# Hymba-style decoder layer on 8 cores: K, V and the forget logits of the first four chunks from an unnormalised x

## The reference, cut to what matters

```
h = rmsnorm(x) * g_mix_pre                     # norm over the 1024 channels
[a_val | a_gate | q | k | v | f_logit] = h @ w_in      # 512 | 512 | 512 | 512 | 512 | 8
A = silu(layernorm(depthwise_conv31(a_val * sigmoid(a_gate))))
B = softmax(q k^T / 8 + sum of log_sigmoid(f_logit + b_forget) over (s, t]) v     # causal, 8 heads x 64
x = x + rmsnorm([A, B] @ w_out)
x = x + rmsnorm((silu(h2 @ w_gate) * (h2 @ w_up)) @ w_down)      # h2 = rmsnorm(x), d_ff 2816
```

## Time and profile before

| | |
|---|---|
| median of 3 runs | 2460.57 us (2458.22 to 2514.89) |
| the profiled execution, its own time | 2455.3 us |
| its span, slowest core (core 7) | 2453.8 us |
| spans of the 8 cores | 2444.3 to 2453.8 us |
| granted TensorE clock, mean | 0.978 |
| busy share: TensorE / ScalarE / VectorE / GpSimd | 92% / 64% / 43% / 21% |

### The profile page before, as it was taken

The page is one execution under the profiler, slowest core; times in us unless marked ns, Lnnn a source line. Parts: engine busy times, 40 slices in busy tenths (PEclk is TensorE's granted clock), DMA queues, the critical chain, the costliest instruction groups (busy, mean ns, idle before and its releaser), DMA issues.

```text
span 2453.8 us, 53606 instructions; the slowest of 8 cores (2444.3 to 2453.8 us)
## 1 busy us (share of the span) xinstructions
PE 2264.7 (92%) x19730; PEld 1078.8 (44%) x19730; DVE 1044.1 (43%) x1638; ACT 1577.3 (64%) x1395; POOL 523.7 (21%) x887
## 2 busy tenths in 40 slices
PE   7988989999999798999999999999999999999895
PEld 3443444444444343444444444444444444444342
DVE  3545455555453533433344243324433432444633
ACT  2246676786776776776777777677777777762211
POOL 0222322322222201230131132023013101302301
PEclk9999999999999899999999999999999999999997
DMA  6766767758769667356445635635563664554542
GB/s 157 192 160 134 187 154 176 186 137 206 164 122 205 159 167 186 108 150 199 129 126 179 178 110 154 206 108 144 165 185 99 169 190 112 151 170 139 160 142 92
DMA packets 226220, 383.76 MB, mean 156 GB/s; under 512 B 34736, under 2 KB 153776, under 8 KB 223920
## 3 DMA queue, kind: packets, MB, share of 16 engines
q1 hardware_dynamic: 192736, 295.98, 42.2%
q0 software_dynamic: 33232, 84.34, 17.1%
HBM read 350.19 MB, written 72.02 MB: 172 GB/s over the span
## 4 chain that ended last, share of the span: by engine, by line
PE 66%; ACT 11%; issue 7%; DVE 7%; DMA 3%; POOL 3%; SPq 1%; DVEq 0%; ACTq 0%; POOLq 0%
PE pbig L470 66%; ACT s_pt L1243 5%; SPq L435 1%; DMA s_kr<-k_s 1%; DVE s_hT L570 1%; ACT s_sq L587 1%; ACT L486 1%; DMA s_xs<-xT 1%; DVE s_tmp L1008 1%; POOL s_pt L1252 1%; ACT s_pt L1248 1%; DVE s_vst L684 1%; ACT s_rstd L486 1%; DMA conv_s<-s_cvst 1%; POOL s_ssA L511 1%
## 5 line engine op out<-in xcount | busy, mean ns | idle before, releaser
L1243 ACT ACTIVATE s_pt<-pbig,s_bias 128x2048 bf16<-128x2048 f32 x512 | 1007.1, 1967 | 426.9 <-PE pbig L470 409.6
L470 PE MATMUL pbig<-s_h,s_wr 128*128 128x512 bf16 x2816 | 671.5, 382 | 15.1 <-DVE s_sa L1075 14.8
L470 PEld LDWEIGHTS pbig<-s_vr,s_pt 128*128 128x128 bf16 x8832 | 345.6, 98 | 167.9 <-issue 48.5
L470 PEld LDWEIGHTS pbig<-s_h,s_wr 128*128 128x128 bf16 x2816 | 253.7, 98 | 375.4 <-issue 119.9
L470 PE MATMUL pbig<-s_vr,s_pt 128*128 128x65 bf16 x8832 | 367.2, 194 | 22.6 <-DVE s_atok L1283 9.8
L470 PE MATMUL pbig<-s_qr,s_kr 64*128 64x512 bf16 x1024 | 308.4, 381 | 60.9 <-ACT s_pt L1243 46.0
L1075 DVE SCALAR_TENSOR_TENSOR s_sa<-s_th,pbig 128x512 f32<-128x512 f32 x176 | 120.9, 687 | 494.8 <-ACT s_th L1074 428.8
L470 PE MATMUL pbig<-s_qw,s_kr 64*128 64x512 bf16 x1024 | 309.9, 383 | 0.0
L1252 POOL TENSOR_SCALAR_AFFINE_SELECT s_pt<-s_pt 128x128 bf16<-128x128 bf16 x256 | 89.6, 350 | 826.5 <-ACT s_pt L1248 792.7
L470 PE MATMUL pbig<-s_actA,s_wr 128*128 128x512 bf16 x1024 | 257.8, 383 | 0.2 <-DVE s_sa L1075 0.2
L511 POOL TENSOR_TENSOR s_ssA<-s_ssA,s_sqr 128x512 f32<-128x512 f32 x98 | 131.6, 1342 | 463.0 <-ACT s_sqr L504 459.2
(11 more groups left out here) (153 smaller groups left out, 2291.3 us busy)
## 6 DMA issues: line engine op xcount, KB each, us to landing
s_wr<-wg_b SPq DMA_DIRECT2D x88, 512.0 KB, 4.0
s_wr<-wu_b SPq DMA_DIRECT2D x88, 512.0 KB, 4.6
s_wr<-wd_b SPq DMA_DIRECT2D x128, 352.0 KB, 3.2
s_vr<-v_s SPq DMA_DIRECT2D x288, 130.0 KB, 3.5
s_kr<-k_s SPq DMA_DIRECT2D x448, 64.0 KB, 3.7
s_xs<-xT POOLq DMA_DIRECT2D x48, 512.0 KB, 7.8
s_u<-u_s POOLq DMA_DIRECT2D x32, 540.0 KB, 12.1
s_x<-xT POOLq DMA_DIRECT2D x32, 512.0 KB, 5.6
```

The source lines that it names most:

```text
L470: P.op("pe", lambda e: e.matmul(out, lhsT=lhsT, rhs=rhs, start=start, stop=stop, **kw), reads=reads, writes=[wkey])
L1243: P.op("act", lambda e: e.activation(out=p[:], in_=pbig[:, 0:4, :], func=AF.Exp, bias=bias[:, c, h:h + 1], scale=1.0), reads=bk + bias.key ...
```

## The change

It does four things.

1. Chunks 0 to 3 get a path of their own, `p_raw`. hT is x * g without r, piece by piece as the pieces come. K is computed with the contraction outermost: for each piece k one matmul of squares and 4 of K, into 5 PSUM banks at once. r is applied when K, V, the logits (and Q and the gates of chunk 1, which reads the same hT) leave PSUM. V and logits have the tokens on partitions, so r is first turned into a column (`rows`: 4 small matmuls and a copy). For chunk 3 hT is made anew with r, for its Q and gates.
2. The K and V weights come in 8 pieces each, the gate weights in 4, and the host lays the gate columns out for that. x pieces of chunks 1 to 3 are loaded singly. vecs, tri and kmask go to ScalarE's queue.
3. The planner no longer counts a transfer that its engine has already waited for; `a_pump` fills one ring slot per step in the wait before a head group.
4. Matmuls that only pass the time: 29 instead of 38.

```diff
         for d in self._deps(eng, reads, writes):
             if d.is_dma:
-                t = max(t, self.landed[d.semkey])
+                if self.clock[eng].get(("dma", d.semkey), 0) < d.dma_n:
+                    t = max(t, self.landed[d.semkey])
...
+    def raw_in(i, k):
+        H = hT[i % 3]
+        P.op("act", lambda e: e.activation(out=sq[:, k, :], in_=xs[:, k, :], func=AF.Square), ...)
+        P.op("dve", lambda e: e.tensor_scalar(out=H[:, k, :], in0=xs[:, k, :], scalar1=V(V_GPRE + k), scalar2=None, op0=ALU.mult), ...)
+        if i + 1 < NRAW:
+            ld("sp", xs, xs[:, k:k + 1, :], xT_d[i + 1, :, k:k + 1, :], reads=winKV.keys[10 + k // 2:11 + k // 2] if i == 0 else (), ...)
+
+    def rows(r):
+        for tb in range(4):
+            mm(pb[0][:, tb:tb + 1], r[:, tb * 128:(tb + 1) * 128], tri[:, 0:1], True, True, r.keys + tri.keys, PB(0))
+        P.op("dve", lambda e: e.tensor_copy(out=rT[:], in_=pb[0][:, 0:4]), ...)
...
+    def p_raw(i, idle):
+        own, j, H, r = i % 2 == 1, i // 2, hT[i % 3], RAW[i]
+        for k in range(8):
+            if i == 0:
+                raw_in(0, k)
+            mm(pb[4][:], ones_bf[:], sq[:, k, :], k == 0, k == 7, ...)
+            for hp in range(4):
+                mm(pb[hp][:], winKV[:, k, hp * 128:hp * 128 + 128], H[:, k, :], k == 0, k == 7, ...)
+            if i == 0 and k < 7:
+                idle(3)
+            yield 5 * MM
+        norm_tail(4, r, 1.0 / D)
+        for hp in range(4):
+            P.op("dve", lambda e, hp=hp: e.tensor_tensor(out=kst[:, hp, :, i % 2, :], in0=pb[hp] ..., in1=r[:] ..., op=ALU.mult), ...)
...
+        else:
+            for tb in range(4):
+                b = bank()
+                yield from group(8, ...)              # V, as before
+                if tb == 1:
+                    rows(r)
+                    v_raw(W, V0, b0, 0)
+                    v_raw(W, V0, b, 1)
+                elif tb:
+                    v_raw(W, V0, b, tb)
+                b0 = b
+                if tb:
+                    for _ in range(2):
+                        if nxt:
+                            raw_in(*nxt.pop(0))
+        yield from logits(i, H, rT)
+        while nxt:
+            raw_in(*nxt.pop(0))
...
     def p_stream():
-        wl("k", winKV, 0, C_K, C_V)
-        for g in range(8):
-            ld("sp", xs, xs[:, g:g + 1, :], xT_d[0, :, g:g + 1, :], ...)
-        ld("sp", vecs, vecs[:], vecs_d)
+        ld("act", vecs, vecs[:], vecs_d)
+        for k in range(8):
+            ld("sp", xs, xs[:, k:k + 1, :], xT_d[0, :, k:k + 1, :], ...)
+        for k in range(8):
+            wk(k, 0, C_K, C_V, winKV.keys[k], ...)
+        for k in range(8):
+            wk(k, 512, C_V, DIN, winKV.keys[8 + k], ...)
...
-        yield from p_kv(0)
-        yield from p_kv(1)
-        flush_h(2)
-        wl("q", winQ, 0, C_Q, C_K, hT[2].keys[0:1])
-        wl("g", winG, 0, 0, C_Q, hT[2].keys[0:1])
+        for i in range(NRAW):
+            yield from p_raw(i, idle)
+            if i == 2:
+                wl("q", winQ, 0, C_Q, C_K, xs.keys[4:5])
+                for cb in range(4):
+                    P.dma("pool", ... winG[:, :, 256 * cb:256 * cb + 256] ..., reads=xs.keys[7:8], ...)
...
+        defer(("h", 3), [scale_by(xs, V_GPRE, rstd, hT[0], k) for k in range(8)], 2, 2)
...
     def gates(j, cb, H, r=None):
+        if r is not None:
+            P.op("dve", lambda e: e.tensor_tensor(out=T[:], in0=pb[bg][:], in1=r[:], op=ALU.mult), ...)
...
+        if r is not None:
+            P.op("dve", lambda e: e.tensor_tensor(out=U[:], in0=T[:], in1=r[:], op=ALU.mult), ...)
...
-            a_pump()
             t0 = fa[0]
             while fa[0] < min(t0 + 18.0, p_end[0]):
+                a_pump(1)
                 yield None
+            a_pump()
```

More of the change, by code:

```diff
@@ L274 @@
 MM = 512 / 2400.0
-EARLY = 1
+NRAW = 4
 NKV = 4
@@ L572, in scale_by @@
             reads=[src.keys[k]] + vecs.keys + r.keys, writes=[dst.keys[k]])
[L574 removed]
+    WK = {"k": lambda k: winKV.keys[k:k + 1], "v": lambda k: winKV.keys[8 + k:9 + k], "q": lambda k: winQ.keys}
+    GK = lambda cb: winG.keys[cb:cb + 1]
+    RAW = {0: rstd, 1: mean, 2: rstd, 3: rstd}
     def proj_T(H, W, c0, b, wk):
[L577 removed]
+        yield from group(8, lambda k: W[:, k, c0:c0 + 128], lambda k: H[:, k, :], pb[b][:], lambda k: (WK[wk](k) if type(wk) is str else wk) + [H.keys[k]], b)
     def flush_h(i):
@@ L588, in norm_sq @@
                                        reads=[xs.keys[k]], writes=[sq.keys[k]]), [xs.keys[k]], "act") for k in range(8)])
[L590 to L604, removed]
+    def raw_in(i, k):
+        H = hT[i % 3]
+        P.op("act", lambda e: e.activation(out=sq[:, k, :], in_=xs[:, k, :], func=AF.Square), reads=[xs.keys[k]], writes=[sq.keys[k]])
+        P.op("dve", lambda e: e.tensor_scalar(out=H[:, k, :], in0=xs[:, k, :], scalar1=V(V_GPRE + k), scalar2=None, op0=ALU.mult),
+             reads=[xs.keys[k]] + vecs.keys, writes=[H.keys[k]])
+        if i + 1 < NRAW:
+            ld("sp", xs, xs[:, k:k + 1, :], xT_d[i + 1, :, k:k + 1, :], reads=winKV.keys[10 + k // 2:11 + k // 2] if i == 0 else (),
+               keys=[xs.keys[k]], sem=("xs0", k))
@@ new lines, in v_fill, with logits @@
+    def v_fill(j, own):
+        W = vst_of(j)
+        if not own and j > 1:
+            P.op("dve", lambda e: e.memset(W[:, :, 4 if j < NOWN - 1 else 0:8, 64:65], 1.0), writes=W.keys)
+        return W, 0 if own else 4
+    def logits(i, H, r=None):
+        bf_ = bank()
+        o = 32 * (i % 2)
+        for tb in range(4):
+            yield from group(8, lambda k: H[:, k, tb * 128:(tb + 1) * 128], lambda k: winKV[:, k, 1024:1032],
+                             pb[bf_][:, tb * 8:tb * 8 + 8], lambda k: WK["v"](k) + [H.keys[k]], bf_, cost=0.033, step=8)
+        if r is None:
+            P.op("dve", lambda e: e.tensor_tensor(out=zt[:, o:o + 32], in0=pb[bf_][:, 0:32], in1=V(V_BF, 32), op=ALU.add),
+                 reads=[PB(bf_)] + vecs.keys, writes=zt.keys)
+            return
+        for tb in range(4):
+            a = o + 8 * tb
+            P.op("dve", lambda e, a=a, tb=tb: e.scalar_tensor_tensor(
+                out=zt[:, a:a + 8], in0=pb[bf_][:, 8 * tb:8 * tb + 8], scalar=r[:, tb:tb + 1], in1=V(V_BF + 8 * tb, 8), op0=ALU.mult, op1=ALU.add),
+                reads=[PB(bf_)] + vecs.keys + r.keys, writes=zt.keys)
@@ L966, in p_own @@
             for cb in range(4):
-                yield from gates(j, cb, H)
+                yield from gates(j, cb, H, r)
                 if cb == 0 and i == 5:
@@ L1188, in build_program, with a_pump @@
     un, uf, qn, qf = [0], [0], [0], [0]
-    def a_pump():
-        while True:
+    def a_pump(n=8):
+        for _ in range(n):
             did = False
```

134 lines of the change are left out of this document (79 added, 55 removed).

## The result

| | before | after |
|---|---|---|
| comparable runs | 2458 to 2461 us | 2431.31, 2435.04, 2437.91 us |
| ratio to before, 95% interval | 1 | 0.9898 [0.9879, 0.9918] |
| first K product of a chunk, mean | 23.8 us | 9.6 us |
| end of chunk 0's logits | 44.9 | 35.6 |
| first Q product | 108.2 | 90.9 |

The change gains 25 us, 1.0%; 2437 was forecast. In the profiled execution of the changed kernel one die's cores ran at a granted clock of 0.92 to 0.93, so it is read on the other die's cores, 4 to 7, and the means of after are over these; those of before and of the experiments are over all eight.

What follows compares the result with a forecast made beforehand. TensorE bounds the kernel (92% busy), with waits and half clock in the first chunks. First Q matmul 24.9 us earlier, less 1 for Q, gates and halo: 24 off 2455.3 gives 2431, plus 5.3 for the median: 2437 us; range 2423 to 2458.

Steps and rivals of the forecast that it cites:

- K of chunk 0: Start: K matmuls go along with the pieces; x and K weights there at about 20.1 us, K done at 22.0.
- B: Rival for the start: weights run ahead of x, x ends at 27.1 us; gain 16, 2444 us; chance 0.12.
- D: Rival: fast hT products on VectorE block GpSimd's descriptors, weights 5 to 6.6 us later; gain 18, 2443; chance 0.05.
- Chunk 1 paced by x: Start: chunk 1's x is read at 35.9 us, TensorE waits about 6 us, K of chunk 1 ends at 37.5.
- Half clock: First four chunks: half-clock stretches, 8 us in all before, cost 3 us with two paced stages left; bounds 0 and 8.
- Q, gates and halo: Chunk 1's stage: extra VectorE work hidden by SyncE's chain of ring fills; 1 us extra, bounds 0 and 5.
- F: Rival: K matmuls between waits keep TensorE at half clock throughout; all four chunks so give 2503 us; chance 0.04.
- G: Rival: nothing gained, the stage ends sooner but its neighbours eat it; 0 to 4 us, 2459; chance 0.05.
- C: Rival: VectorE becomes the bound in chunks 2, 3 and the gates, gate weights late; gain 11, 2450 us; chance 0.10.
- The rest at 0: From the first attention matmul on: same work in another order, taken as 0; bound 17 us either way.
- E: Rival: the later order, through the planner's two landed conditions, gains or loses 17 us: 2420 or 2454; chance 0.05 each.
- A: Main case, all terms as summed: gain 17 to 31 us, 2430 to 2444; chance 0.54.

Runs made afterwards that it cites:

- e4: Changed kernel without the passing products within K of chunk 0 (idle(3) to idle(0)); ratio to before 0.9905 [0.9882, 0.9927].
- e11: Changed kernel with one passing product per piece of chunk 0 instead of three, and its V tiles drained in order 0, 3, 1, 2; 2427.79 us, ratio to before 0.9875.
- e12: e11 with two columns of r fewer: chunks 2 and 3 take chunk 1's column; 2428.0 us, ratio 0.986 [0.980, 0.992].
- e6: Changed kernel with chunk 0's forget logits in PSUM bank 0 instead of the bank whose V tile leaves last; ratio to before 0.9920 [0.9907, 0.9933].
- e7: Changed kernel without the eight products that normalise chunk 3's hT (its Q and gates come out wrong); ratio to before 0.9896 [0.9878, 0.9915].
- e8: Changed kernel with ring fills issued in one go as before, the planner's new condition kept; ratio to before 0.9900 [0.9884, 0.9916].
- e2: Changed kernel with the planner's condition and the spread ring fills taken back; median 2439.7 us, ratio to before 0.9921 [0.9895, 0.9947].
- e5: Kernel before with one number changed: the scheduler's sum of projection work starts at 1.7067 us (8 products) instead of 0; ratio 0.9959 [0.9946, 0.9972].

## Why the prediction was right, and where it was not

The time came out right by luck: two errors in the sum, of 9 and of 7 to 12 us, went opposite ways.

- **K of chunk 0: right on core 7, 2.7 us late over the cores.** 22.90 and 24.7 against 22.0. On core 7 x was complete at 18.4 with all sixteen weight pieces queued beside it, so B (weights ahead of x) did not happen. The Trainium skill (DMA: Bandwidth & Descriptors, "Queues, rings and completion order") has each DMA engine alternate between queues; the trace agrees, x being complete at 18.4 beside the weights. There is no sign of D either: the sixteen issues took GpSimd 8.87 us, 0.55 each, while hT products ran at 0.49. But of the 23 us, 4.5 were passing products: they, not x, set the pace on core 7. With fewer of them the weight pieces set it (e4, e11).
- **V and logits of chunk 0: wrong by 2.9 us** (10.8 instead of 7.9). Left out were the wait for a PSUM bank (2.13, shown by e11) and the column.
- **Chunk 1 paced by x: wrong.** x's last piece was squared at 35.4, as forecast (35.9), but TensorE reached chunk 1 only at 33.71 and then needed its own 8.6 us: 42.3 instead of 37.5. Even by the forecast's own 29.9 for the end of the logits it could not have been done before 38.5. A stage ends by the later of arrival and work; I had let the work run ahead of its own start.
- **Column of r: mis-sized.** 0.1 us forecast; the row says 0.81 and e12 0.7. They are fp32 products, 8 instructions where the source has 4.
- **VectorE's wait in chunk 2: right in kind.** 2 us forecast; 0.63 and 1.42 measured, but for PSUM banks instead of hT pieces.
- **Half clock: too careful on core 7, half right elsewhere.** 3 us forecast. On core 7 there is none after 13 us; on cores 5 and 6 it costs 1.4 us in chunk 1, behind the bank wait of 2.13 us. Where that wait was 0.43 us (e11, e12) no core had it there, where it was 4.31 (e6) all had. That the passing products hold it off is not shown.
- **First Q product**: on core 7 83.6 forecast, 88.33 found; over the cores 17.3 us earlier instead of 24.9. Three of these 7.6 us lie in the cores: on core 7 the first K product ran at 8.27, on cores 5 and 6 at 10.67 and 10.46, with the first Q product at 93; one core alone hid that. 1.4 of it is the half clock of chunk 1.
- **Q, gates and halo: the named cause was wrong, and the term was half of what it measured.** 1 us more was forecast and 2.1 measured (39.1 against 37.0). I had TensorE wait for SyncE's chain; it waited for VectorE (2.22 us at 115.18), and e7 gave 1.4 of it back.
- **The signs named beforehand.** Met: clock 1.00 on core 7 over 40 to 70 and 50 to 100 us, hT product between its two prices, no wait for winQ or winG, the conv input's store 17.4 us behind the first ring fill (101.23 to 118.59), the rest within 17 us (2294.7 on core 7). Missed: first Q product at 80 to 88 (88.33), first attention near 121 to 122 (127.70), and the first real matmul before 10 us on cores 5 and 6 (10.67 and 10.46). F and G, the half clock throughout and no gain, did not occur; C is in part what binds the gates.
- **The rest at 0: wrong by 12 us in the profile and by 7 over the comparable executions, inside its bound of 17.** This was rival E's better half, but not for E's reason. E named the planner's `landed` conditions. They reorder a few heads and give 2 us between heads 8 and 16, of which e8 has nothing left at head 32. The lasting part, 8 to 10 us from head 32 on, comes from the ledger's 8 products, and is there without those conditions (e2) and without the new start (e5). A and E's half together made the number: the sum's error of 9 us and this one nearly cancel.

## What to carry to other kernels

Where a planner orders the work, price a local edit twice: by what it does on the spot, and by shifting the planner's own sums alone, as one number in the old kernel; here that alone gave 10 of 25 us. When several accumulations leave PSUM together, go through what is asked for next and in which bank it lands, in the order of the draining engine's queue: freeing a bank earlier for one user can hand a longer wait to the next (e6). And matmuls that pass the time should be tried at several counts, with nothing else changed: here none and three gave the same time (e4), and one was run only together with another edit (e11).

## What the runs showed of the hardware

- Eight fp32 products of one column, each with its own stationary tile, hold TensorE 0.81 us until the next product starts; eight bf16 products of 512 columns take 1.72.
- Sixteen weight pieces of 128 or 130 KB cost GpSimd 0.55 us each to issue (8.87 in all), and in the changed kernel only the first was waited for on core 7 (1.39 us); as two whole loads the same weights made TensorE wait 10.88 us.
- The granted clock is best read with the duration of a product beside it: over 10 to 20 us core 5 of e11 shows 1.00, and yet four products of 512 columns took 1.86 us at 11.28, as at half clock.
- The first weight piece arrives at another time on each core: the first K product of the kernels with pieces ran anywhere from 7.9 to 11.3 us; the cause was not looked for.
